# Last expert's weights in finer pieces, and one piece of expert 14 sent as three transfers

## The reference

```
proj = h @ w_in                                  # z, xBC, dt, u, gates
y_a  = bidirectional SSD scan (conv, silu, gated RMS norm) @ w_out
y_b  = bidirectional complex S5 scan, gelu, gated linear unit
h    = LN(alpha * h + (sigmoid(g_a) * y_a + sigmoid(g_b) * y_b) @ w_o)

aff       = softmax(h @ w_router)                # 16 experts
gate, idx = top_k(aff.T, 64)                     # each expert chooses 64 tokens
xin = h[idx]
hid = silu(xin @ w_e1) * (xin @ w_e3)            # 1024 -> 2816
y   = (hid @ w_e2) * gate                        # 2816 -> 1024
out = LN(alpha * h + scatter_add(y))
```

## Time and profile before

| | |
|---|---|
| median of 3 runs | 2069.79 us (2068.78 to 2072.78) |
| profiled execution | 2070.14 us |
| its span | 2068.4 us |
| TensorE matmul busy | 1890.5 us (91%) |
| VectorE, ScalarE, GpSimd busy | 673.8, 394.8, 289.7 us |
| moved by DMA | 638.16 MB, mean 309 GB/s |
| chain of waits | PE 48%, DMA 39% |

### The profile page before, as it was taken

How to read it: one execution, slowest core, us unless ns; L and a number is a source line. 1 busy time by engine, 2 the same in 40 slices (tenths; PEclk the granted TensorE clock), 3 DMA queues, 4 the chain that set the end, 5 groups by cost and what they waited for, 6 DMA issues and landing times.

```text
span 2068.4 us, 20135 instructions
## 1 busy us (share of the span) xinstructions
PE 1890.5 (91%) x8454; PEld 932.6 (45%) x8454; DVE 673.8 (33%) x1170; ACT 394.8 (19%) x708; POOL 289.7 (14%) x284
## 2 busy tenths in 40 slices
PE   8999999999999997999888989988988988988987
PEld 4656578566678753333323333333333333323332
DVE  6599869798865352001000000100100100100103
ACT  1434322289710031000000000000000000000001
POOL 1696533165300000000000000000000000000001
PEclk9899999999999998999999999999999999989999
DMA  5622313233333577999999999999999999999995
GB/s 145 140 81 72 117 55 113 76 123 122 108 145 111 217 301 293 404 428 435 431 432 431 431 432 431 432 431 431 432 430 432 431 431 432 430 431 432 431 423 239
DMA packets 78954, 638.16 MB, mean 309 GB/s; under 512 B 19932, under 2 KB 33680, under 8 KB 60816
## 3 DMA queue, kind: packets, MB, share of 16 engines
q1 hardware_dynamic: 66224, 628.99, 74.2%
q10 hardware_dynamic: 12640, 7.89, 1.3%
HBM read 626.98 MB, written 9.88 MB: 308 GB/s over the span
## 4 chain that ended last, share of the span: by engine, by line
PE 48%; DMA 39%; DVE 3%; ACT 1%; issue 1%; SPq 0%; DVEq 0%
PE ps L1134 47%; DMA arena<-in_w_e 39%; ACT arena L778 1%; DVE arena L1984 1%; ACT L778 0%; DVE arena L1981 0%; PE ps L1636 0%; PE ps L1245 0%; DVE arena L2306 0%; DVE arena L2271 0%; PE ps L1388 0%; DVE arena L2300 0%; DVE arena L2206 0%; DVE arena L2208 0%; PE ps L1524 0%
## 5 line engine op out<-in xcount | busy, mean ns | idle before, releaser
L1134 PE MATMUL ps<-arena 128*64 128x512 f32 (+9 forms) x7856 | 1814.9, 520 | 138.9 <-DMA arena<-in_w_e 122.5
L1134 PEld LDWEIGHTS ps<-arena 128*64 128x64 f32 (+2 forms) x7856 | 861.4, 159 | 1060.9 <-issue 863.9
L778 ACT ACTIVATE arena<-ps 128x512 f32<-128x512 f32 (+5 forms) x305 | 169.5, 581 | 1524.2 <-PE ps L1134 895.9
L2271 DVE TENSOR_TENSOR arena<-arena,ps 128x512 f32<-128x512 f32 (+1 forms) x48 | 30.1, 644 | 691.3 <-PE ps L1134 691.3
L770 POOL TENSOR_TENSOR arena<-arena 128x1024 f32<-128x1024 f32 x3 | 7.0, 2350 | 1348.9 <-ACT arena L778 1348.9
L2280 DVE TENSOR_TENSOR arena<-arena,ps 128x512 f32<-128x512 f32 x48 | 33.1, 690 | 402.3 <-PE ps L1134 402.3
L778 ACT ACTIVATE arena<-arena 128x128 f32<-128x128 f32 (+10 forms) x261 | 118.4, 509 | 97.6 <-DVE arena L1984 36.9
L778 ACT ACT_TABLE_LOAD x74 | 94.9, 1283 | 29.8 <-issue 24.7
L1984 DVE SCALAR_TENSOR_TENSOR arena<-arena 128x512 f32<-128x512 f32 x80 | 67.9, 849 | 2.8
L703 POOL TENSOR_TENSOR arena<-arena 128x768 f32<-128x768 f32 x16 | 28.4, 1778 | 82.8 <-DVE arena L2035 49.0
L1636 PE MATMUL ps<-arena 128*128 128x128 f32 x176 | 25.7, 295 | 7.0 <-DVE arena L2271 5.9
(11 more groups left out here) (220 smaller groups left out, 778.4 us busy)
## 6 DMA issues: line engine op xcount, KB each, us to landing
arena<-in_w_e SPq DMA_DIRECT2D x76, 5632.0 KB, 29.3
arena<-in_w_e SPq DMA_DIRECT2D x15, 2816.0 KB, 26.4
arena<-in_w_e SPq DMA_DIRECT2D x26, 1408.0 KB, 15.6
arena<-in_w_in SPq DMA_DIRECT2D x9, 2048.0 KB, 8.6
arena<-in_w_e SPq DMA_DIRECT2D x12, 1536.0 KB, 16.7
arena<-cumulative_scratch SPq DMA_DIRECT2D x16, 768.0 KB, 5.0
arena<-in_w_in SPq DMA_DIRECT2D x5, 1536.0 KB, 6.5
arena<-in_w_out_ssd SPq DMA_DIRECT2D x4, 1536.0 KB, 6.7
```

Source lines behind the costliest of these rows:

```text
L778: return act.activation(out, in_, func, **kw)
L1134: return pe.matmul(out, lhsT, rhs, start=a, stop=z)
L2271: tt(o, o, ps[:, 3 + i, 0:w], ALU.mult).then_inc(s.hid_ready, 1)
```

## The change

Three places. The cuts of the last expert: w_e1's second half becomes two pieces of two rows, w_e3 becomes one piece per row, and the last piece of w_e2 (two rows) becomes two. The first piece of expert 14 (rows 0 to 3 of w_e1, 5632 KB) is sent as three transfers instead of one: partitions 0 to 111, 112 to 119 and 120 to 127, all counted on the same semaphore, for which `piece_landings` now counts transfers. And the four `sum_so_far` behind row 3 of w_e3 are issued one each behind rows 2, 3, 4 and 5.

```diff
-        (EXPERTS - 1, 1): [0, 2, 4] if j == 0 else [0, 2, 3, 4], (EXPERTS - 1, 2): [0, 3, 6, 9, 11]}.get((x, w), [0, RUN[w]])
+        (EXPERTS - 1, 0): [0, 4] if j == 0 else [0, 2, 4], (EXPERTS - 1, 1): [0, 1, 2, 3, 4], (EXPERTS - 1, 2): [0, 3, 6, 9, 11] if j == 0 else [0, 3, 6, 9, 10, 11]}.get((x, w), [0, RUN[w]])
...
-        piece_landings = [i // LANDINGS + 1 for i in range(len(PIECES))]
+        STRIPS = ((0, 112), (112, 120), (120, 128))
+        strips = lambda i: STRIPS if i == piece_of[EXPERTS - 2, 0, 0, 0] else ((0, P),)
+        piece_landings = [sum(len(strips(v)) for v in range(i % LANDINGS, i + 1, LANDINGS)) for i in range(len(PIECES))]
...
-                sp.dma_start(arena[:, piece_place[i]:piece_place[i] + piece_size[i]], src).then_inc(piece_loaded[i % LANDINGS], 16)
+                for p0, p1 in strips(i):
+                    sp.dma_start(arena[p0:p1, piece_place[i]:piece_place[i] + piece_size[i]], src[p0:p1]).then_inc(piece_loaded[i % LANDINGS], 16)
...
-                    if k == 3 and which and x + 1 == EXPERTS:
+                    if 2 <= k < 6 and which and x + 1 == EXPERTS:
                         pe.wait_ge(s.silu_half, 3 * EXPERTS)
-                        for c in range(2):
-                            for j in range(2):
-                                sum_so_far(c, j)
+                        sum_so_far(*divmod(k - 2, 2))
```

## The result

| | before | after |
|---|---|---|
| median of 4 runs each | 2070.82 us (2068.78 to 2072.78) | 2099.48 us (2098.34 to 2099.57) |
| ratio | 1 | 1.0136 [1.0124, 1.0148] |
| profiled execution, span | 2070.14, 2068.4 us | 2099.40, 2097.6 us |

The forecast was 2078.6 us, between 2067.5 and 2085.0. The direction was right; the size was far outside the range.

A forecast was written before the change was run, and what follows sets the result against it. DMA was taken as the bound until the last expert, where TensorE and DMA end almost together. Cuts -0.2 and the three transfers +9.0 gave +8.8 us: median 2078.6 us, range 2067.5 to 2085.0.

The forecast's parts named there:

- Cuts, -0.2 us: Last expert: finer pieces and spread sums alone end the kernel 0.2 us earlier, between -1 and +0.7.
- 112 partitions are seven stretches for each of 16 engines: Expert 14's first piece: the wide transfer splits evenly over all engines at their full rate, 11.7 us.
- the upper bound of +15: Expert 14's piece: largest shift of later landings allowed, with no lead used and some collision.
- the lead: Eight of 16 engines finish 8 to 9 us before the last one, taken as unused slack.
- the collision with the neighbours: Following pieces write to the same 16 partitions, stretching the narrow transfers from 13.4 us to 19 to 20.
- The transfers of 8, 13.4 us on their engines: Expert 14's two narrow transfers: 6.7 us per stretch in place of 1.67, on each of eight engines.
- the U loads: Eight traced loads of 16 partitions each, 104 to 111 GB/s, taken as guide to narrow transfers' rate.
- The lead covers most of it, 8 to 9 us off the sum: Expert 14's piece: early engines' slack absorbs most of the narrow transfers' +11.7 us, leaving 3 us.
- The chain: Chain of waits: the DMA step of 30.29 us ending at 1925.70 becomes 39 us, later ones unchanged.
- rivals 1 and 2: Engine's rate decides at expert 14; the eight lead (2067.9 us, chance 0.15) or are behind (2071.3 us, chance 0.06).
- a positive D: Landings behind expert 14's split piece move later; +9 us was taken, within -1.67 to +15.
- Rival 3: Expert 14's narrow transfers are slow and on the engines behind, nothing covered: +13, 2082.6 us, chance 0.15.

The follow-up runs named there:

- the fenced kernel: Changed kernel with SP waiting for the landing before the three transfers and for theirs behind them: 2097.30 against 2071.42 us for the kernel before.
- the row of 3.3 us that cost 10: Kernel before with one row of expert 14's first w_e1 half cut off and sent as 64 + 64 partitions: 2082.53 against 2072.04 us.
- The fence that took the lead away: Changed kernel with SP waiting for the previous piece's landing ahead of the three transfers, nothing behind: 2096.34 against 2072.92 us for the kernel before.

## Why the prediction was wrong

**Cuts, -0.2 us.** Right within what can be measured (1.0002 [0.9994, 1.0011], so -1.2 to +2.3 us). The 1.89 us went and a wait came in their place; I had said a few tenths, it was 0.91 us.

**"112 partitions are seven stretches for each of 16 engines", 11.7 us.** This is the step that failed. Alone the transfer takes 21.0 us. I had written that it may collide too and that the trace shows no such transfer, and then gave this no price beyond the upper bound of +15. I spread its bytes evenly over the engines and forgot that where the engines write decides. In the sum this is 9.3 of the missing 19.9 us (7.9 without the start, which a transfer in the flow doesn't pay); the lead, below, is another 8 to 9. The two of 8 give 1.9 back. The rest is the collision with the neighbours: the forecast had 6 us for it, and an estimate from the fenced kernel is 28.9 - 19.3 = 9.6.

**The transfers of 8, 13.4 us on their engines.** Nearly right: 5.8 + 5.7 us alone. The nearest row, the U loads, was a good guide. But "on each of their eight engines" was wrong: while they are under way the core takes in 145 GB/s at a share of 0.97. Eight engines untouched would alone bring 8 x 27 = 216 GB/s. With nothing beside them the transfers of 8 bring 61 GB/s, which leaves 84 for the others, 10.5 each. So the other eight were slowed too.

**The lead covers most of it, 8 to 9 us off the sum.** Wrong in sign. The engines ahead enter the slow transfer early and slow those behind, which are the ones that set each landing. The piece before the split shows it, 8.4 us late with a lead of 7.1 to 8.3, and the row of 3.3 us that cost 10. The fence that took the lead away without making it worse agrees.

**The chain.** A step of 39 us was expected in place of 30.29; it is 49.27, and the one before it is 38.63 already, since the piece that was still arriving was slowed as well. That the later steps stay as they were held: the last 21.98 us are there again. So did the dip that was to show rivals 1 and 2 wrong (from 1875 instead of 1880), but over some 50 us and not 20 to 30. The share of 0.50 at the end shrank, as said for a positive D.

**The rivals.** None held. Rival 3, the dearest, had +13; all of them took the wide one at the full rate of its engines. Rival 3 doesn't add up either: with the 6 us of collision that the forecast itself uses and nothing covered it is 11.7 + 6 = 17.7, above my bound of 15 and still below what was measured. The bounds went wrong in the same place: for the 112, an operation that no row shows, I took no end from a row. The nearest are the U loads, 107 GB/s with all 16 engines at work. At that rate 112 partitions (5.05 MB) are 47 us. However far, that end would have kept the measured time inside.

## What to carry to other kernels

Send large tiles as transfers of all 128 partitions and split them by rows, not by partitions: every partition split of one 5.6 MB piece cost 18 to 32 us, the finer rows of the last expert nothing that could be measured. In these runs a transfer that is badly spread slowed whatever else was in flight, so price it as a slow stretch for all engines, which begins when the first engine enters it and ends when the last leaves it. And where engines show a lead, ask what it will run into before it is counted as cover.

## What the hardware showed that was not expected

- Sixteen engines that are all busy can move half of the full rate: share 0.93 at 199 GB/s for 96 partitions, against 0.94 at 387 for 128.
- Engines that share no place, by the port map, are held to the pace of those that do (partitions 16 to 79: share 0.92 over 14.7 us, 3.5 us for a stretch on all 16 engines).
- Partitions 32 to 95 came in at 352 GB/s, 0 to 63 at 187: as many bytes, 32 partitions further on.
- A transfer of 96 partitions takes longer (21.6 us) than one of 128 (14.8 us) of the same rows.
- Of 128 partitions the page "DMA: Bandwidth & Descriptors" of the Trainium skill, section "The descriptor swizzle", says that each engine writes one port only. The 433 GB/s before and behind every slow stretch agree with it, also while engines are 8 us apart.
